# Two transformer blocks on one NeuronCore: the exchange of row groups for the rotary angles, by TensorE's products or by transfers on GpSimd's queue

## The reference, cut to what matters

```
z = n @ mix_w_in[l]                       # n: modulated rmsnorm of h
zq, zkv, zg, zuv, zga, zgb = split(z)     # 8 query heads of 64, 6 key/value kinds of 2 groups, ...
q  = rope(zq);  ks = rope(k_sel);  kw = rope(k_win)
kc = rope(compress(k_cmp))                # 31 compressed keys
y_a = gates * (attention over kc, over ks blocks, over the kw window)
y_b = u * (W_s v + b),   u, v = split(gelu(zuv)),  v layer-normed
h = h + mod * ((sigmoid(zga) * (y_a @ proj_a) + sigmoid(zgb) * (y_b @ proj_b)) @ w_out)

rope(x):  x1, x2 = split(x, 2, axis=-1)   # the two halves of a head's 64 values
          return concat([x1 * cos - x2 * sin, x1 * sin + x2 * cos])
```

## Time and profile before

| | us |
|---|---|
| median of 3 runs | 3289.78 |
| lowest, highest | 3289.11, 3290.45 |
| the profiled execution | 3289.11 |
| its span | 3287.3 |

### The profile page before, as it was taken

The page is one execution under the profiler, slowest core; times in us unless marked ns, Lnnn a source line. Parts: engine busy times, 40 slices in busy tenths (PEclk is TensorE's granted clock), DMA queues, the critical chain, the costliest instruction groups (busy, mean ns, idle before and its releaser), DMA issues.

```text
span 3287.3 us, 51926 instructions
## 1 busy us (share of the span) xinstructions
PE 3242.4 (99%) x22014; PEld 2741.6 (83%) x22014; DVE 2175.8 (66%) x3567; ACT 1461.7 (44%) x2496; POOL 118.7 (4%) x211
## 2 busy tenths in 40 slices
PE   8999999999999999999999999999999999999998
PEld 6878767888888888888778899989998877789997
DVE  6575764678666665665654677767776666467776
ACT  5233565335344422234553444454444455344443
POOL 1000000101000010100000000000000000000000
PEclk9999999999999999999999999999999999999999
DMA  4010103665544365643112232333323321222322
GB/s 155 26 59 31 39 27 96 223 192 184 183 147 147 111 240 193 240 158 108 57 46 87 81 115 85 110 97 97 108 91 115 111 81 47 82 84 91 115 91 83
DMA packets 101751, 364.40 MB, mean 111 GB/s; under 512 B 11776, under 2 KB 13888, under 8 KB 100880
## 3 DMA queue, kind: packets, MB, share of 16 engines
q1 hardware_dynamic: 77040, 272.14, 25.7%
q0 software_dynamic: 24480, 88.95, 8.3%
HBM read 358.94 MB, written 2.10 MB: 110 GB/s over the span
## 4 chain that ended last, share of the span: by engine, by line
PE 92%; DVE 5%; ACT 2%; issue 0%; DMA 0%; POOL 0%; DVEq 0%; ACTq 0%; POOLq 0%
PE ps_run L479 91%; PE ps_run L871 1%; DVE wl L2245 1%; ACT nrm L1368 1%; ACT wh L1368 0%; DVE nrm L2245 0%; DVE X L2252 0%; DVE nrm L2252 0%; PE ps_run L1218 0%; DVE HL L2252 0%; DVE msk L2249 0%; ACT bias L1368 0%; ACT HH L1368 0%; DVE L L2475 0%; DVE kn L2252 0%
## 5 line engine op out<-in xcount | busy, mean ns | idle before, releaser
L2245 DVE TENSOR_TENSOR wl<-st,wh 128x1024 fp32r<-128x1024 f32 (+1 forms) x565 | 687.5, 1218 | 531.4 <-ACT wh L1368 531.2
L479 PE MATMUL ps_run<-HH,wh 128*128 128x512 f32 (+1 forms) x2560 | 911.2, 356 | 11.0 <-DVE HL L2252 3.2
L479 PE MATMUL ps_run<-HH,wl 128*128 128x512 f32 (+1 forms) x2560 | 893.6, 349 | 0.0
L479 PE MATMUL ps_run<-HL,wh 128*128 128x512 f32 (+1 forms) x2560 | 891.4, 349 | 0.0
L1368 ACT ACTIVATE wh<-st 128x1024 fp32r<-128x1024 f32 (+1 forms) x565 | 591.1, 1048 | 539.6 <-PE ps_run L479 426.3
L479 PEld LDWEIGHTS ps_run<-HH,wh 128*128 128x128 f32 x2560 | 485.0, 189 | 82.6 <-DVE HL L2252 5.9
L479 PEld LDWEIGHTS ps_run<-HL,wh 128*128 128x128 f32 x2560 | 485.2, 190 | 63.0 <-issue 3.8
L479 PEld LDWEIGHTS ps_run<-HH,wl 128*128 128x128 f32 x2560 | 484.8, 189 | 63.3
L479 PE MATMUL ps_run<-AH,wh 128*128 128x512 f32 (+1 forms) x1152 | 444.6, 386 | 1.2 <-DVE AL L2245 1.2
L479 PE MATMUL ps_run<-AL,wh 128*128 128x512 f32 (+1 forms) x1152 | 438.4, 381 | 0.0
L479 PE MATMUL ps_run<-AH,wl 128*128 128x512 f32 (+1 forms) x1152 | 438.2, 380 | 0.0
(11 more groups left out here) (456 smaller groups left out, 4070.8 us busy)
## 6 DMA issues: line engine op xcount, KB each, us to landing
st<-wst SPq DMA_DIRECT2D x511, 512.0 KB, 3.7
mb<-ada POOLq DMA_DIRECT2D x144, 512.0 KB, 4.8
cw<-cw POOLq DMA_DIRECT2D x4, 1024.0 KB, 6.3
X<-xT SPq DMA_DIRECT2D x8, 256.0 KB, 4.9
X<-xT POOLq DMA_DIRECT2D x8, 256.0 KB, 4.4
out<-X SPq DMA_DIRECT2D x16, 128.0 KB, 1.8
kc<-kc POOLq DMA_DIRECT2D x1, 1073.5 KB, 7.0
mb<-cond POOLq DMA_DIRECT2D x2, 512.0 KB, 6.9
```

Source lines behind the costliest of these rows:

```text
L479: i = self.e.matmul(out, lhsT, rhs, start=start, stop=stop, skip_group_check=True)
L2245: self.e.tensor_tensor(out, a, b, op).then_inc(*self.w.done(*points))
```

## The change

x goes to two buffers in turn (`Vs[0:2]`) and the exchanged x to two others (`Vs[2:4]`); these tiles receive the values only at the end of the stage. GpSimd's queue copies four groups of 32 partitions, 64 KB each, from one to the other. ScalarE's copy waits for the turned tile two before rather than one before, and its first copy of values into Vs waits for kw's. VectorE multiplies x by the cosine first, straight into the output tile, then waits for the last of the four transfers. TensorE's six products a mixer are gone; kc keeps its own.

```diff
@@ Memory
+        self.rope_x, self.rope_r = self.Vs[0:2], self.Vs[2:4]
@@ Pe.mixer
-        def turn(name):
-            self.rope((key, name), "perm64", m.nrm[0], 512, turns)
-
-        def lin(name, cols, before=None):
-            line = self.linear((key, name), fe(cols, *nm, 8), m.HH, m.HL, None, dense)
-            next(line)
-            if before is not None:
-                turn(before)
-            finish(line)
+        def lin(name, cols):
+            finish(self.linear((key, name), fe(cols, *nm, 8), m.HH, m.HL, None, dense))
...
-        for k, _ in enumerate(self.wide((key, "gv"), vw, m.HH, m.HL, None, wide)):
-            if k in (0, 2, 4):
-                turn(("q", k // 2))
+        finish(self.wide((key, "gv"), vw, m.HH, m.HL, None, wide))
...
-        lin("ks", c128(kv + 256), ("q", 3))
+        lin("ks", c128(kv + 256))
...
-        lin("kw", c128(kv + 512), "ks")
+        lin("kw", c128(kv + 512))
...
-        turn("kw")
@@ Act.mixer
         def rope_x(k):
-            if k:
-                w.wait_ge("turned", (key, ropes[k - 1]))
+            if k >= 2:
+                w.wait_ge("turned", (key, ropes[k - 2]))
             else:
                 w.wait_ge("lo", f"m{l}", 15)
-            self.rope_x((key, ropes[k]), (key, ropes[k]), m.nrm[0], scale=0.125 if k < 4 else 1.0)
+            self.rope_x((key, ropes[k]), (key, ropes[k]), m.rope_x[k % 2], scale=0.125 if k < 4 else 1.0)
...
             w.wait_ge(key, "v", tb)
+            w.wait_ge("turned", (key, "kw"))
             self.act(m.Vs[tb][:, 0:256], b[:, 0:256], ACT.Copy)
@@ Dve.mixer
         def turned(k):
-            self.turned((key, names[k]), 512, m.nrm[0], m.nrm[1], m.cos2, m.sin2, outs[k])
+            x, r, of = m.rope_x[k % 2], m.rope_r[k % 2], (key, names[k])
+            w.wait_ge("rope x", of)
+            self.tt(outs[k], x, m.cos2, MUL)
+            w.wait_ge("swapped", of)
+            self.tt(r, r, m.sin2, MUL)
+            w.own()
+            self.tt(outs[k], outs[k], r, ADD, ("turned", of))
@@ Pool.mixer
+        for k, name in enumerate([("q", i) for i in range(4)] + ["ks", "kw"]):
+            x, r, of = m.rope_x[k % 2], m.rope_r[k % 2], (key, name)
+            w.wait_ge("rope x", of)
+            for p in (0, 32, 64, 96):
+                q = p ^ 32
+                self.load(r[p:p + 32, :], x[q:q + 32, :], f"swap{l}{k % 2}", *([("swapped", of)] if p == 96 else []))
         w.wait_ge(key, "heads act")
```

## The result

The changed kernel took 3302.3 us (median of 6 runs, 3300.85 to 3302.84), the kernel before 3289.6 beside it on the same chip. The ratio is 1.0038, with a 95% interval of 1.0025 to 1.0051: slower by 12.7 us. The forecast was 3289.4 us, and the range ended at 3298.0.

The account below looks back on a forecast made before the run. TensorE, busy for 99% of the span, was taken to bound the kernel. From 3289.11 us, 11.1 us gross came off and 10.8 us of new waiting came on, giving 3289.4 us; range 3283 to 3298.

Parts of the forecast that it names:

- What goes: TensorE's six exchanges a mixer, 0.85 us each, plus 0.45 us idle before ks: 5.55 us a mixer, 11.1 in all.
- What comes, VectorE's and GpSimd's work: VectorE's two products and sum, and GpSimd's 24 transfers a mixer, were to add no cost; the price was latency.
- The cover of the first three: Exchanges q0 to q2: transfers covered, q0 late by 0.5 us at most, gain 2.55 us a mixer.
- A = 0.1 + 1.53 + 2.45: End of ScalarE's x copy to fourth landing: release, issues, landing; 4.1 us, bounds 3.4 and 5.9.
- The chain through VectorE and ScalarE: At q3 and ks each engine's order passes lateness on: q3 late by 1.34 us, ks by 3.55.
- The new wait at kw's bank: TensorE waits about 5.7 us before rq,yT for ScalarE's kw copy to free a PSUM bank, in each mixer.
- From there to the end of the stage, 11.45: From kw's copy end to the end of the values: 12.30 us before, less kw's exchange of 0.85.
- The hidden wait for kw's landing: VectorE's split behind kw's landing comes late, but TensorE does not wait for that slab up to A = 6.1.
- The first (all 11.1 us gained): Rival: bank or ScalarE's order does not hold TensorE, giving 3278.0 us; chance 0.13 together with the costless-landing case.
- The transfers of a batch hold each other up: Rival: the four transfers delay one another, landing 4.3 us, A = 5.9, time 3296.7 us; chance 0.20.
- GpSimd's lock: Rival: GpSimd cannot write descriptors while VectorE works; batch 2.0 us late, A = 6.1, time 3297.4 us; chance 0.07.
- What would show it: Signs: TensorE idle 5 to 6 us before rq,yT, VectorE waits about 2 us for q3, ks, kw, landings 2.45.

Follow-up runs that it names:

- e4: Changed kernel with VectorE's wait, sine product and sum moved behind the next gate-value steps (q3, ks) or slab split (kw): 3277.46 us, ratio 0.9959.
- e6: Changed kernel with transfers for q0 to q2 only, TensorE's products back for q3, ks and kw: 3285.24 us, ratio 0.9986.
- e1: Changed kernel with the three slab loads released by splits V0 to V2 held until q3, ks and kw are turned: 3293.03 us, ratio 1.0007.
- e10: Changed kernel with sixty unused products of 280 columns added on TensorE ahead of rq,yT: 3298.68 us, ratio 1.0026.
- e3: Changed kernel with rq,yT in the free PSUM bank 3 in place of the bank kw holds: 3299.85 us, ratio 1.0029.
- e2: Changed kernel with VectorE's wait for the transfers put ahead of the cosine product: 3305.09 us, ratio 1.0042.
- e8: Changed kernel with e4's late sine products, e3's bank and e1's held loads together: 3279.03 us, ratio 0.9963.
- e7: Changed kernel with eight transfers of 16 partitions in place of four of 32: 3306.9 us, ratio 1.0049.

## Why the prediction was wrong

*What goes.* Right. The 24 products and their time are gone; e4 gives the whole gross gain once nothing waits, and e6 the three covered exchanges at 4.8 us against 5.1.

*What comes, VectorE's and GpSimd's work.* Right: 2175.4 us of VectorE beside 2175.8, and the queue's issues cost nothing by themselves.

*The cover of the first three.* Right in what it gains (e6), but thinner than I had it. VectorE waited 2.01 us for q0's transfers and took up the sine product at 1486.03, 5.05 us behind the copy, where before it was 3.66: late by 1.4 us and not by 0.5. The split behind it came at 1487.66 and still waited 0.21 us for ScalarE, so nothing was lost. q1 and q2 did not wait.

*A = 0.1 + 1.53 + 2.45.* **This is the step that failed.** The issues were right (1.47 for 1.53). The release took 0.28. The landing took 4.1 to 4.4 where I took 2.45. The sentence "SP's queue has nothing moved; its slab loads only share the DMA engines" named the cause and gave it no price. Those loads are issued the moment VectorE's split ends, and the split stands right ahead of the exchange, so the third and fourth transfer of every late batch met one. The bound of 4.3 was in the text, from the 32 KB pieces beside a slab load; taking the middle of the two nearest rows passed over what the upper bound said of the situation, which was this one. With the landing taken from that row the sum would have been 3296.7. With the release, A was 2.04 us longer than I had it, which is 4 x 2.04 = 8.2 us.

*The chain through VectorE and ScalarE.* Right, with the formulas. At A = 6.14, q3 should be late by A - 2.76 = 3.38. VectorE was free at 1530.58, not 1528.30, though q3's copy came 1.12 us earlier than before (1522.50, not 1523.62), so it was late by 3.40. For ks 2A - 4.65 = 7.63, measured 7.55.

*The new wait at kw's bank.* Right in place, releaser and both mixers; 9.2 us where the same working gives 2.15 + 7.6 = 9.8.

*From there to the end of the stage, 11.45.* **This term was wrong as well:** it was read from a TensorE that had not stood still. After 9.2 us of idle the granted clock was 0.50, which cost 1.6 and 2.7 us. In e1 waits of 5.0 and 4.9 us cost 2.4 and 2.2, so the forecast 5.7 us would most likely have cost as much. Even with the landing as I took it, the time would have been some 4.5 us above 3289.4 (an estimate from e1). Neither mistake alone leaves the range: the late landing gives 3297.6, the clock with a timely landing some 3294.

*The hidden wait for kw's landing.* It was hidden up to A = 6.1 by my working. For kw A was 6.08 in mixer 1 and 7.17 in mixer 2 (VectorE waited 5.24 us there, the fourth transfer took 5.4). No wait of TensorE for the split is seen in the changed kernel, whose values were themselves slowed by the clock. In two runs the wait does come out: 0.49 us in mixer 2 of e10, where the clock stayed up, and 1.68 and 1.18 in e3, with the other bank.

*The rivals.* The first (all 11.1 us gained) fell with the 9.2 us of wait, and came true in e4, where what spoke against it had been taken out. "The transfers of a batch hold each other up" has its size, A = 5.9, but not its mechanism: in e1 the same batch lands in 1.9 to 2.1. GpSimd's lock has the other size that fits, A = 6.1. Against it stand the pitch of 0.49 us, the first issue 0.28 after the copy, the quick landing of the second transfer, which is issued beside VectorE's split, and e2, in which the late two stay late beside an idle VectorE.

*The sum.* 3289.11 + 4 x 6.14 - 16.1 = 3297.6; the clock makes it 3301.9; the start of that execution adds 1.5. The profiled execution took 3302.84.

*What would show it.* Of the signs I named, "landings of 4 and more is the batch rival" would have misled a reader, since two causes give that number. Nor does one batch tell them apart, as late transfers would be slow under both. What does is where the border falls in different batches (behind the second transfer for q3, ks and kw, behind the first for q2, each time at the end of the split), and e1. And VectorE's waits were 4.1 to 4.2 us in mixer 1, where I had named 2.

One thing stays open: whether the third transfer lost to the load at the DMA engines alone, or also on its way there. It was issued at 1524.36, before the load could go at 1524.43, and was served behind it.

## What to carry to other kernels

Work that is replaced by a transfer is paid in latency, and the latency is paid by whatever stands behind the wait in its engine's order: put the independent work between issue and use first. In e4 neither the landing nor what it met mattered after that. Price a small transfer by what other queues issue shortly before and beside it, not by its size alone. Where a sum leaves TensorE standing for 5 us and more, add what the lower clock costs behind it.

## What the runs showed of the hardware

- A transfer of 64 KB within SBUF, on GpSimd's queue, landed in 1.8 to 2.1 us with no load beside it (e1, the three batches of mixer 1; 1.8 to 2.6 in mixer 2). In the changed kernel it took 4.1 to 4.4 when a load of 512 KB was issued on SyncE's queue at about the same time, and the load itself 4.1 to 4.4. For kw in mixer 2 it was 5.4, with a load of 5.6.
- Ahead of the load the border is not sharp. Issued 0.6 us ahead of it, the second transfers of q3, ks and kw in mixer 1 took 1.9 to 2.0, but kw's in mixer 2 took 4.1. Issued 0.3 to 0.4 ahead there are 1.9 (e4, ks's fourth) and 3.2 (e8, ks's second), and 0.1 ahead it is 4.1 to 4.3.
- Behind the load the landing shortens with the load's age. q0's first three transfers, issued some 0.7, 1.4 and 1.9 us behind a load that took 4.2, landed in 3.2, 2.7 and 2.4, that is 3.9 to 4.3 us behind that load's issue. That is the picture of something which has to get past a fixed obstacle, as e7 has it.
- Waits of 5.0 and 4.9 us at rq,yT cost 2.4 and 2.2 us of lowered clock behind them (e1), waits of 9.2 cost 1.6 and 2.7. So between 5 and 9 us the loss did not grow with the length of the idle. Waits of 1.5 and 1.3 us behind a busy stretch left the granted clock at 1.00 in both mixers (e10).
